# Row exponentials moved to the end of a convolution, and sixteen weighted sums moved from two GEMMs into a value product

## What is computed

```python
m_lat = ada_modulation(c, ada_w[l], ada_b[l])        # silu(c) @ w + b, split in 6 rows of 2048
hl = modulate(rmsnorm(x_lat, norm_mix[l]), m_lat[0], m_lat[1])
pl = hl @ w_in[l]                                    # 2048 x 5648
ql, kl, vl, gl = mlstm_inputs(...)                   # q, k: silu(3-tap convolution), 1024 wide
h_l, _ = mlstm_bidir(ql, kl, vl, gl, ctx_states, True)
y_l = stream_mixers(pl, h_l, rows, GRID_W, *mix_args)
x_lat = x_lat + m_lat[2] * (y_l @ w_out[l])
hf = modulate(rmsnorm(x_lat, norm_ffn[l]), m_lat[3], m_lat[4])
x_lat = x_lat + m_lat[5] * peer_ffn(hf, peer_wq[l], peer_keys[l], peer_u[l], peer_v[l])
return rmsnorm(x_lat, norm_final)
```

## Time and profile before

| | us |
|---|---|
| median of 3 runs | 3143.62 (3141.54 to 3150.24) |
| profiled execution | 3157.12, its span 3155.3 |
| lat gemm, 176 chunks | 1096 to 1368.7 |
| start of the mLSTM | 1368.7 to 1433.5 |
| units ci=0, update, units ci=1 | 1433.5 to 1482 |
| mix_out gemm | 1490 to 1590 |
| wq gemm, choice of experts | 1597 to 1747 |
| experts | 1747 to 2418 |
| value product | 2422.8 to 3141 |

### The profile page before, as it was taken

The page is one execution under the profiler, slowest core; times in us unless marked ns, Lnnn a source line. Parts: engine busy times, 40 slices in busy tenths (PEclk is TensorE's granted clock), DMA queues, the critical chain, the costliest instruction groups (busy, mean ns, idle before and its releaser), DMA issues.

```text
span 3155.3 us, 39929 instructions
## 1 busy us (share of the span) xinstructions
PE 2994.9 (95%) x12354; PEld 2188.0 (69%) x12354; DVE 2373.6 (75%) x4369; ACT 1872.6 (59%) x4178; POOL 307.0 (10%) x372
## 2 busy tenths in 40 slices
PE   8999999999999999988987799899999999999998
PEld 6888888888887888776776233333334888888886
DVE  6788777888868568866858899999997555555556
ACT  5655545555556765454455688787787555555554
POOL 1000000000000000000000333333331000000000
PEclk9999999999999999978999555555556999999999
DMA  7667767777776558940844899999998555555554
GB/s 260 213 213 227 220 235 239 241 245 242 244 244 227 174 173 286 374 167 21 300 135 155 359 413 411 383 405 411 412 421 356 189 188 189 188 187 186 186 186 147
DMA packets 214208, 792.95 MB, mean 251 GB/s; under 512 B 17410, under 2 KB 18130, under 8 KB 151458
## 3 DMA queue, kind: packets, MB, share of 16 engines
q1 hardware_dynamic: 159040, 408.99, 39.9%
q0 software_dynamic: 51344, 370.53, 29.8%
q10 hardware_dynamic: 3668, 11.53, 1.0%
HBM read 783.64 MB, written 7.34 MB: 251 GB/s over the span
## 4 chain that ended last, share of the span: by engine, by line
PE 66%; DVE 18%; DMA 10%; ACT 2%; issue 2%; DVEq 1%; ACTq 1%; POOL 0%; POOLq 0%
PE bank L496 12%; PE bank L498 12%; PE bank L497 12%; DVE u_ring L2569 8%; DMA u_ring<-in_peer_u,idx 8%; PE bank L2745 7%; PE bank L2747 7%; PE bank L2746 7%; DVE u_more L2569 3%; DVE raw_lo L486 1%; DVE acc L551 1%; DMA ada_ring<-in_ada_w 1%; PE bank L854 1%; ACT hi L480 1%; DMA raw<-in_w_in 1%
## 5 line engine op out<-in xcount | busy, mean ns | idle before, releaser
L480 ACT ACTIVATE hi<-raw 128x512 fp32r<-128x512 f32 x1008 | 600.5, 627 | 451.4 <-PE bank L498 252.5
L486 DVE TENSOR_TENSOR raw_lo<-raw,hi 128x512 fp32r<-128x512 f32 x1008 | 658.9, 690 | 254.8 <-ACT hi L480 251.2
L496 PE MATMUL bank<-hi,xt_hi 128*128 128x512 f32 x1632 | 655.8, 402 | 24.5 <-DVE raw_lo L486 24.2
L498 PE MATMUL bank<-hi,xt_lo 128*128 128x512 f32 x1632 | 638.0, 391 | 0.0
L497 PE MATMUL bank<-raw_lo,xt_hi 128*128 128x512 f32 x1632 | 638.0, 391 | 0.0
L2499 PE MATMUL bank<-row_ring,one_row 96*128 96x512 bf16 x1024 | 529.2, 621 | 54.5 <-DVE act_in L2569 25.3
L2668 DVE TENSOR_TENSOR w_lo<-v_raw,w_hi 128x512 fp32r<-128x512 f32 x496 | 343.4, 693 | 292.3 <-ACT w_hi L2641 289.9
L2641 ACT ACTIVATE w_hi<-v_raw 128x512 fp32r<-128x512 f32 x496 | 313.1, 632 | 330.8 <-PE bank L2747 330.8
L2569 DVE CUSTOM_DVE_ANT_0 u_ring<-u_ring,bank 128x1024 f32<-128x1024 f32 x344 | 405.7, 1216 | 29.7 <-DMA u_ring<-in_peer_u,idx 18.0
L2745 PE MATMUL bank<-w_hi,vw_hi 128*128 128x512 f32 x992 | 395.2, 398 | 3.0 <-DVE w_lo L2668 3.0
L2746 PE MATMUL bank<-w_lo,vw_hi 128*128 128x512 f32 x992 | 394.9, 398 | 0.0
(11 more groups left out here) (453 smaller groups left out, 3497.8 us busy)
## 6 DMA issues: line engine op xcount, KB each, us to landing
v_raw<-in_peer_v SPq DMA_DIRECT2D x128, 1024.0 KB, 4.8
ada_ring<-in_ada_w POOLq DMA_DIRECT2D x96, 1024.0 KB, 7.1
raw<-in_w_in_ab SPq DMA_DIRECT2D x128, 512.0 KB, 3.8
raw<-in_w_in_c SPq DMA_DIRECT2D x128, 512.0 KB, 4.0
raw<-in_w_in SPq DMA_DIRECT2D x120, 512.0 KB, 3.7
raw<-in_w_out_ab SPq DMA_DIRECT2D x32, 512.0 KB, 4.3
raw<-in_w_out_c SPq DMA_DIRECT2D x32, 512.0 KB, 4.4
raw<-in_w_out SPq DMA_DIRECT2D x32, 512.0 KB, 6.3
```

What stands on the lines that cost most here:

```text
L480: act.activation(hi[:, c % HI, :], raw[d % RAW][:, c % KC, :], ACT.Copy).then_inc(hi_ready, 1)
L486: dve.tensor_tensor(raw_lo[d % RAW][:, c % KC, :], raw[d % RAW][:, c % KC, :], hi[:, c % HI, :].bitcast(F32), ALU.subtract).then_inc(lo_sp ...
L496: pe.matmul(o, a_hi, b_hi, start=kk == 0, stop=False, skip_group_check=True)
L498: last = pe.matmul(o, a_lo, b_hi, start=False, stop=kk == K - 1, skip_group_check=True)
```

## The change

The row exponentials. `row_exps_act(act, 1)` stands behind the convolution instead of in its blocks 7 to 10. `ml_cols_pe` moves from i=13 into `unit_pe` of ci=0, behind the first two exponents, and writes bank 5. The copy to `col` moves into `unit_dve`, and ACT waits for it ahead of its first `from_state`, PE ahead of `weighted(1)`. The second chunk's scores are split: one head behind each of the first four `from_state`.

```diff
-            for k in range(K):
-                load(80 + k, 5, k)
...
-            for c in (2 * i, 2 * i + 1):
-                kk = c % K
-                last = pe.matmul(bank[:, 0, c:c + 1], acc[c // K][:, kk * P:(kk + 1) * P], ones[:, 0:1], start=True, stop=True)
...
-                for i in range(28):
-                    if s == 72 + i * 11 // 3:
...
+                if s >= 70 and (s - 70) % 6 == 0 and s <= 160:
+                    i = (s - 70) // 6
+                    modulate(dve, 56 + i, 0, *((8 + i, 0) if i < 8 else (i - 8, 3)))
...
-                if i == 13:
-                    ml_cols_pe(pe)
...
-                if 7 <= i < 11:
-                    next(exps, None)
-                    next(exps, None)
                 if i >= 13:
                     keys_cols_act(act, i - 13)
+            for _ in row_exps_act(act, 1):
+                pass
...
             exponent(0)
             exponent(1)
             if ci == 0:
-                scores_pe(pe, 1)
+                ml_cols_pe(pe)
             for j in range(8):
                 from_state(j)
+                if ci == 0 and j < MH:
+                    scores_pe(pe, 1, (j,))
...
+                if 50 <= s < 58 and s % 2 == 0:
+                    scale_cols_pe(pe, (s - 50) // 2)
...
-                if s % 4 == 0 and 12 <= s < 60:
-                    modulate(dve, 84 + (s - 12) // 4, 0, 4 + (s - 12) // 4, 3)
-            dve.drain().then_inc(row_summed, 1)
+                if s % 5 == 0 and 10 <= s <= 45:
+                    modulate(dve, 72 + (s - 10) // 5, 0, 8 + (s - 10) // 5, 3)
+                if s == 60:
+                    scale_cols_dve(dve)
...
-            sum_row_pe(pe, 3)
...
-            take_row_act(act, 1)
...
+            pool.wait_ge(gate_stored, 16)
+            for half in (slice(0, P // 2), slice(P // 2, P)):
+                pool.dma_start(gate_cols[:, half, :], gate_rows[half, :].rearrange("p (j c) -> j p c", c=K)).then_inc(gate_turned, 16)
...
-            sp.dma_start(x[:, :, :], x_rows.rearrange("(t p) d -> p t d", p=P)).then_inc(x_back, 16)
...
+                        if c == 1 and isinstance(m, int) and GATE_FROM <= m < GATE_TO:
+                            gate_half_dve(dve, 4 * (m - GATE_FROM) + j)
+                    if j == 1 and isinstance(m, int) and m == FOLD_AT:
+                        gate_fold_dve(dve)
```

More of the change, by code:

```diff
@@ L547, in modulate @@
             o = acc[to][:, :]
-            if to < 2 and k == 0:
+            if to != 2 and k == 0:
                 done = dve.tensor_scalar(o, ada_ring[:, i % 2, :], c_col[:, v, 0:1], None, ALU.mult)
@@ L1031, in sum_cols_dve, with shift_cols_pe, shift_cols_dve, scale_cols_pe @@
             dve.tensor_tensor(m_col[:, v * 6 + g, :], bank[:, 7 - v, o:o + K], ada_bias[:, g, :], ALU.add)
-        def last_cols_pe(pe, i):
-            if i == 0:
-                pe.wait_ge(ada_used, PRE + 80)
-                pe.wait_ge(u_gated, 1)
-            for c in (2 * i, 2 * i + 1):
-                kk = c % K
-                last = pe.matmul(bank[:, 0, c:c + 1], acc[c // K][:, kk * P:(kk + 1) * P], ones[:, 0:1], start=True, stop=True)
-            if i == K - 1:
+        def shift_cols_pe(pe, kk):
+            if kk == 0:
+                pe.wait_ge(ada_used, PRE + 64)
+                pe.wait_ge(u_gated, 1)
+            last = pe.matmul(bank[:, 0, kk:kk + 1], acc[0][:, kk * P:(kk + 1) * P], ones[:, 0:1], start=True, stop=True)
+            if kk == K - 1:
+                last.then_inc(acc_summed, 1)
+        def shift_cols_dve(dve):
+            dve.wait_ge(acc_summed, 5)
+            dve.tensor_tensor(m_col[:, 3, :], bank[:, 0, 0:K], ada_bias[:, 3, :], ALU.add)
+        def scale_cols_pe(pe, part):
+            if part == 0:
+                pe.wait_ge(ada_used, PRE + 80)
+                pe.wait_ge(lo_written, PRE + NG * 5)
+            for kk in range(4 * part, 4 * part + 4):
+                last = pe.matmul(bank[:, 4, kk:kk + 1], acc[3][:, kk * P:(kk + 1) * P], ones[:, 0:1], start=True, stop=True)
+            if part == 3:
                 last.then_inc(acc_summed, 1)
-        def last_cols_dve(dve):
-            dve.wait_ge(acc_summed, 5)
-            for g in (3, 4):
-                dve.tensor_tensor(m_col[:, g, :], bank[:, 0, (g - 3) * K:(g - 2) * K], ada_bias[:, g, :], ALU.add)
+        def scale_cols_dve(dve):
+            dve.wait_ge(acc_summed, 6)
+            dve.tensor_tensor(m_col[:, 4, :], bank[:, 4, 0:K], ada_bias[:, 4, :], ALU.add)
             dve.drain()
@@ L1662, in ml_cols_pe, with scores_pe @@
                     for t in range(T):
-                        o = 64 + q * 16 + d * 8 + t * 4
-                        pe.matmul(bank[:, 0, o:o + 4], rows[n][:, d, t * P:(t + 1) * P], eye[0:MH, 0:MH], start=True, stop=True)
+                        o = q * 16 + d * 8 + t * 4
+                        pe.matmul(bank[:, 5, o:o + 4], rows[n][:, d, t * P:(t + 1) * P], eye[0:MH, 0:MH], start=True, stop=True)
             pe.wait_ge(decays_spread, 2)
-            pe.matmul(bank[:, 0, 112:128], ones[0:MH, :], decay_x[:, :, :].rearrange("h c n -> h (c n)"), start=True, stop=True).then_inc(ml_a, 1)
+            pe.matmul(bank[:, 5, 48:64], ones[0:MH, :], decay_x[:, :, :].rearrange("h c n -> h (c n)"), start=True, stop=True).then_inc(ml_a, 1)
         def scores_of(t, hh):
             return bank[:, 2 + t, hh * P:(hh + 1) * P]
-        def scores_pe(pe, t):
+        def scores_pe(pe, t, heads=range(MH)):
             tok = slice(t * P, (t + 1) * P)
-            for hh in range(MH):
+            for hh in heads:
                 for b in range(2):
@@ L1797, in weighted @@
                 pe.wait_ge(ml_weighted, u0 + j + 1)
+                if ci == 0 and j == 1:
+                    pe.wait_ge(coefs_taken, 3)
                 pe.matmul(bank[:, 4 + j % 2, 0:MD + 1], p_t[j % 2][:, :], v_one[:, t, hh, :], start=True, stop=True).then_inc(ml_mixed, 1)
@@ L1826, in unit_act @@
                     act.wait_ge(ml_stated, u0 + j + 1)
+                    if ci == 0 and j == 0:
+                        act.wait_ge(coefs_taken, 3)
                     act.activation(from_state[j % 2][:, :], bank[:, 6 + j % 2, 0:MD + 1], ACT.Copy, scale=coef(1, d, t, hh)).then_inc(ml_scaled, 1)
@@ L2592, in bass_hybrid_stack_kernel @@
         ADDS_AT = 8
+        GATE_FROM, GATE_TO, FOLD_AT = 2, 10, 20
         def passes_of_blocks(eng, body):
             body(0, True)
-            with eng.Fori(0, NK // 4 - 2) as i:
-                body(i + 1, False)
+            for m in range(1, GATE_TO):
+                body(m, False)
+            with eng.Fori(0, FOLD_AT - GATE_TO) as i:
+                body(i + GATE_TO, False)
+            body(FOLD_AT, False)
+            with eng.Fori(0, NK // 4 - 2 - FOLD_AT) as i:
+                body(i + FOLD_AT + 1, False)
@@ new lines, in gate_half_dve @@
+        def gate_half_dve(dve, n):
+            k, o = n // 2, slice(n % 2 * (D // 2), (n % 2 + 1) * (D // 2))
+            i = 80 + k
+            dve.drain()
+            dve.wait_ge(ada_landed[i % 2], 16 * (i // 2 + 1))
+            if k == 0:
+                done = dve.tensor_scalar(acc[3][:, o], ada_late[:, i % 2, o], c_kept[:, 0:1], None, ALU.mult)
+            else:
+                done = dve.scalar_tensor_tensor(acc[3][:, o], ada_late[:, i % 2, o], c_kept[:, k:k + 1], acc[3][:, o], ALU.mult, ALU.add)
+            if n % 2:
+                done.then_inc(ada_used, 1)
```

67 lines of the change are left out of this document (42 added, 25 removed).

## The result

The changed kernel takes 3132.4 us (median of 11 runs, 3127.5 to 3139.7), the kernel before 3143.9 (11 runs, 3140.3 to 3150.2). The ratio is 0.9959, with a 95% interval from 0.9947 to 0.9970, so 12.9 us less by the ratio, between 9.4 and 16.7 (11.5 by the two medians alone).

The account below looks back on a forecast made before the run. PE bounds the value product; elsewhere PE's gaps come largely from waits for DVE, in the two gemms and the convolution. Gains of 3.0 + 4.8 + 1.1 + 0 + 0 = 8.9 us take 3143.6 to 3134.7 us, range 3125 to 3150.

Parts of the forecast that it names:

- the first rival: Clock already up when the mLSTM's units begin: gain there 8.7 us in place of 4.8, 3130.5 us with upper ends elsewhere; chance 0.17.
- The convolution: Start of the mLSTM: without eight table exchanges and ACT's waits in blocks 7 to 10, scores begin 13.6 us earlier.
- The units: mLSTM units: first one 11.4 us earlier, part given back to second scores at half clock; gain 4.8 us, bounds 3.1 and 8.7.
- the middle case: mLSTM units: PE's clock rises at 1430.5, so they end at 1443.6, 5.8 us earlier, before 1 us for a hand-over.
- The lat gemm: Lat gemm: twelve modulates and two memsets fewer on DVE remove PE's waits for low halves; gain 3.0 us, bounds 0 and 3.2.
- mix_out: mix_out: fewer waits for low halves gain 5.0 us, column sums on PE cost 3.9; net +1.1, between -1.8 and +2.2.
- wq, experts, value product: End of wq zero, as PE next waits for the choice of experts; nothing of the change in the experts; value product zero.
- the halves: Value product: 32 half modulates for the gate on DVE, 1.28 us each, covered by a 2.85 us lead; zero cost.
- Clock up early: Rival: PE's clock is up when the mLSTM's units begin, gain 8.7 us there in place of 4.8; chance 0.17.
- Clock down through the units: Rival: PE's clock stays at half through the first mLSTM units, time 3146.9 us, or 3150 with the update; chance 0.12.
- the gain isn't there: Rival: the gemms' waits move to the loads and the units swallow the convolution's gain, 3143 us; chance 0.07.
- The value product pays: Rival: the gate's 64-byte transfers make the fold late, 3250 us at 150 ns a piece, or low halves come late; chance 0.09.

## Why the prediction was right or wrong

**Right for the sum and for the mechanism of its largest term; short in the lat gemm.** 8.9 us forecast, 12.9 measured. By the total alone the first rival, which gave 13 us and 3130.5, would fit better than the forecast; only the stages tell them apart. By its steps:

*The convolution.* Forecast: scores 13.6 us earlier; the profiles: 13.6 on average (41.6 us after the gates against 55.2). On ACT after, at the end of the convolution:

```profile
1411.01 0.42 ACT L1637 ACTIVATE q_t<-conv 128x256 f32<-128x256 f32 x1 [0.32 <-DVE conv L1624]
1411.33 0.58 ACT L1662 ACTIVATE h<-bank 128x512 f32<-128x512 f32 x1
1411.92 1.28 ACT L1586 ACT_TABLE_LOAD   x1
1413.22 0.42 ACT L1586 ACTIVATE row_wk<-row_f 4x256 f32<-4x256 f32 x1
...
1414.56 0.71 ACT L1594 ACTIVATE row_i<-row_th 4x256 f32<-4x256 f32 x2
```

One table load, 1.30 us to the next ACTIVATE (1.29 in the earlier trace rows), and all exponentials done at 1415.3, ahead of PE's need. From block 8 on DVE waits for ACT's scaling by 0.4 us at most, where it was up to 3.27. The 2.66 us for an exchange that the Trainium skill gives ("ScalarE: Activation LUTs", What ACT_TABLE_LOAD costs) don't appear here either.

*The units.* Forecast: the first unit 11.4 us earlier, the end of the units 4.8. PE after:

```profile
1411.47 3.78 PE L1683 MATMUL bank<-q_t,k_t 128*128 128x128 f32 x16 [2.77 <-ACT q_t L1637]
...
1417.06 1.70 PE L1671 MATMUL bank<-eye_sb,row_wk 4*128 4x4 f32 x8
...
1422.55 2.08 PE L1792 MATMUL bank<-h,q_t 128*128 128x257 f32 x4
1424.42 1.06 PE L1683 MATMUL bank<-q_t,k_t 128*128 128x128 f32 x4
...
1427.58 1.92 PE L1792 MATMUL bank<-h,q_t 128*128 128x257 f32 x4
...
1431.46 1.03 PE L1792 MATMUL bank<-h,q_t 128*128 128x257 f32 x4
...
1446.10 4.38 PE L1761 MATMUL bank<-v_weighed,h 128*128 128x257 f32 x12 [2.30 <-DVE h L1871]
```

Two units begin 5.03 us apart with the head's scores at half clock (forecast 4.95), and from 1431.46 on `from_state` takes 1.03. The clock rose at about 1430.2, next to the 1430.5 that I had taken, and the 1 us that I had charged for a hand-over ahead of the first unit isn't there: PE goes from the small transposes into the unit without a wait. Counted from the gates, the first unit is 12.0 us earlier than in the earlier trace rows, the update 6.6; over all profiles 6.0 for 4.8. The choice of the middle case was a guess that came out on average; the profiles of one form differ by up to 6 us in this stretch, with the clock.

*The lat gemm.* Forecast 3.0, measured 5.5; the sign was right and the step was too narrow: it put the waits down to DVE's load per chunk and took their 3.2 us as the most that could be gained. DVE's load is real, but its share is the short delays, some 1.7 us that the list of waits leaves out. The waits that I did read the earlier trace rows were the long ones, and what a modulate's own late load or a late weight chunk adds to them I had as the lower bound, 0 "if they come from loads of the ring". That bound had it backwards, since because loads are part of it, taking 12 MB away helps; the sentence behind it, that twelve loads fewer speak for the upper end, pointed the right way and got no price. And 3.2 us was one execution's value; the long delays, which come to somewhat more than the gaps in the list, ran from 0.4 to 7.5 in five profiles.

*mix_out.* Forecast +1.1 net; from the turning of the blocks to the norm it is 114.4 in the old form and 113.1 in the new on average, +1.3, and from the update 1.2. The net came out by some luck. Short waits of 2.2 us stayed beside the start, where 0.7 was foreseen, so the list fell by 3.4 and not by 5.0; the long delays of PE, summed as in the table of the lat gemm, fell by 4.0, the wait at the norm 0.3 (7.29 to 6.96), and the columns cost 3.8, which leaves 0.8 of the 1.3 unaccounted for. The clock held during the column sums, which at 0.95 us a piece were priced right. The error was to look for the price of the columns and not for a free place for them: the wait of about 7 us at the norm is in both profiles.

*wq, experts, value product.* -0.1 for 0 and, from the experts, 0.8 that nobody forecast and that isn't explained; the halves 0 for 0. The fold cost PE 1 us in place of 0 to 0.5, since the reduction of 128x2048 took 3.70 us and not 2.4:

```profile
2864.24 3.70 DVE L2633 TENSOR_REDUCE gate_sum<-gate_cols 128x16 f32<-128x2048 f32 x1
```

```profile
2869.40 0.47 PE L2805 MATMUL bank<-w_hi,vw_hi 128*128 128x512 f32 x1 [0.98 <-DVE w_lo L2723]
```

*The rivals.* "Clock up early" did come, in two of eight profiles: from 1420 to 1430 PEclk was 0.83 and 0.71 in them, where the profile shown has 0.50, and the update came 70.5 and 71.5 us after the gates, 9 to 10 us earlier than before, where the rival said 8.7. "Clock down through the units" came in none, and "the gain isn't there" is out by the interval. "The value product pays" is out: the gathers were issued at 2638.6 and 2651.4 and landed after 11.2 us each,

```profile
gate_cols<-gate_rows POOLq DMA_DIRECT2D x2, 512.0 KB, 11.2
```

some 200 us ahead of the fold. My price of 84 us for both was nearly four times too high. The Trainium skill ("DMA: Bandwidth & Descriptors", Specifications) has 512 bytes as the smallest transfer at line rate. The trace agrees: with pieces of 64 bytes, 512 KB in 11.2 us are 47 GB/s, where 1 MB of `v_raw` in 4.8 us is 218, and with 224 us of time it made no difference.

## What to carry to other kernels

A wait names who released it, not who was late: follow it back over the engines, and to part compute from transfers put the compute back without them. Compare that profile with those of its form that had no long wait, since delays too short for the list of waits can add up to as much as the effect. A pair of profiles can differ by more than the change is worth (here they differ by 19.4 us, and the change is worth 12.9), so compare stages that both kernels share as well, and take a second profile of the kernel before ahead of explaining a stage that nobody edited. Small jobs of a bound engine belong in its own longest wait.

## What the runs showed of the hardware

The spacing of back-to-back matmuls of 512 columns in the value product has two values, 0.2289 and 0.2333 us, at a granted clock of 1.00 throughout. It kept its value for as long as PE wasn't held up. In the profile with the doubled halves it was 0.2333 from the start and 0.2289 from the fold on, where PE waited once for about 1 us; that is the one change within a stage that was seen, and in the profiles at 0.2289 the same wait changed nothing. Of 14 profiles, the first two of the kernel before and this one had the slower value; the last part, which takes its weights from another place, had 0.2268 after either. What sets it at the start of a stage stays open, and whether timed runs have it as often as profiled ones can't be seen.
